# Scan products of an S5/short-convolution layer: high and low parts side by side, two parts of four groups

## Chip, cores and metric

One core of a Trainium2 chip. The metric is the device time of one execution in microseconds (us). The kernel before ran three times: median 1619.18 us, 1614.2 to 1620.25.

## What is computed

One layer over 576 tokens (a prompt of 512 and eight samples of eight), model width 2048. An input projection gives eight streams. One of them, u (1024 wide, 64 groups of 16 channels), drives a state space with 64 complex states per group; the other parts are a gated convolution and gates. Cut to what matters here:

```python
proj = jnp.einsum('bld,dn->bln', x, w_in)
u_a, z_a, b_c, c_c, h_c, z_c, g_a, g_c = jnp.split(proj, SPLIT_POINTS, axis=-1)
bu = einsum('blgc,gpc->blgp', u_groups, b_bar)          # input to the states
h = associative_scan(...)                               # h_t = lam * h_(t-1) + bu_t
y = einsum('blgp,gcp->blgc', h_re, c_re) - einsum('blgp,gcp->blgc', h_im, c_im) + d * u
y = gelu(y); y = y * sigmoid(y @ w_glu)
merged = sigmoid(g_a) * ((y * silu(z_a)) @ w_out_a) + sigmoid(g_c) * (conv_part @ w_out_c)
y_out = layernorm(alpha * x + merged @ w_o)
```

## The kernel before

**Main products.** Every float32 product is made of three in the one-pass type float32r: with high and low parts of both sides, hi*hi, hi*lo and lo*hi are added in PSUM. The weights come as 264 "halves" (128 output features by 1024 inputs; the last 32 pass a second time). Per half h, SyncE loads `w_raw`, ScalarE copies the high part (`split`, L736), VectorE subtracts to get the low part (`split`, L947), and TensorE issues 48 matmuls of 288 columns (`half`, L618: 8 blocks of 128 inputs, 3 products, 2 token halves). `lo_ready` lets TensorE into a half, `half_done` is incremented at its end, and ScalarE and VectorE run their own copies of the loop over h. In step h each of them first makes the parts of half h + 2, then reads the accumulator of the half that ends with this step (if its turn comes), and only then does the scan's steps: `scan_steps(h)` stands last in every iteration. An engine's queue is strictly in program order.

**The scan.** The 64 groups go in 8 blocks of 8 groups. Tokens are cut in chunks of T = 8, so a block's tokens are 72 columns per group. A block b begins every 16 halves, and `ssm_step(h, off)` says at which distance `off` from a block's begin a step falls. The blocks run beside halves 16 to 159: the first 64 of these are the convolution's (L1293, four blocks begin there), the next 16 the gate z_a's (L1328), the last 64 the merge gates' (L1341). Of a block:

- off 4, 5: high and low parts of the matrices and of u (`lcl` L1204, `lbl` L1210, `ul` L1213);
- off 7, before half 7: TensorE's `states_in` (L637 to L639), for each group lbh*uh, lbh*ul and lbl*uh of 72 columns into `v_ps`, 24 in all, then 16 narrow ones for the filter taps (L646); ScalarE copies `v_ps` to `v_st` (L774) in its step 7; VectorE goes on with it in step 8 (`chunk_sums`);
- off 9 to 17: rotation, scan, rotation back, high and low parts of the states (`hh`, `hl`);
- off 19, before half 19: TensorE's `outputs` (L658 to L663), six products of 72 columns per group into `y_ps`, 48 in all; ScalarE copies `y_ps` to `y_pre` (L757);
- off 20 to 24: GELU on VectorE and ScalarE (L1228, L1229, L792, L1233), and the store.

The accumulator readers that matter: in the convolution, at off 3 and 11 (mod 8: 3) VectorE waits for `half_done(h + 1)`, the end of the half that is running, and makes q (L1304 to L1308); at 5 (mod 8) it waits likewise and multiplies (L1318); at 7 (mod 8) ScalarE makes the sigmoid (L831) and VectorE two products (L1323, L1325), again after that half's end. In z_a's halves, every odd h has ScalarE's sigmoid (L841) and VectorE's product (L1335) after the half's end; in the merge gates' halves every odd h has ScalarE's sigmoid (L854) there, and VectorE has nothing of the kind.

Of the kernel before, what the change touches and what calls it, by code (L numbers as in the profile page):

```python
# [5 lines left out]
F32 = mybir.dt.float32  # L6
# [88 lines left out]
def build(nc, d):  # L95
# [52 lines left out]
    u_raw = r("u_raw", [P, NG, CH])  # L148
    uh = r("uh", [P, NG, CH], F32R)
    ul = r("ul", [P, NG, CH], F32R)  # L150
    lbh = r("lbh", [P, NG, 2 * STATE], F32R)
# [12 lines left out]
    y_pre = r("y_pre", [P, NG, CH])  # L164
    hh = r("hh", [P, NG, CH], F32R)
    hl = r("hl", [P, NG, CH], F32R)
    k_st = r("k_st", [P, 2, T * GC])
# [8 lines left out]
    out_st = [r(f"out_st{i}", [P, TOK]) for i in range(4)]  # L176
    st = u_raw

    r = Region(s0)
# [57 lines left out]
    def halves_of(ps):  # L237
        return ps[:, :, 0:TH]
# [17 lines left out]

    def by_bank(t):
        return t[:, :, :].rearrange("p (t g) n -> p t (g n)", t=2)

# [41 lines left out]
    k_done = sem("k_done")  # L301
    v_evac = sem("v_evac")
    k_evac = sem("k_evac")
    v_ready = sem("v_ready")
# [11 lines left out]
    y_done = sem("y_done")  # L316
    y_evac = sem("y_evac")
    y_arg = sem("y_arg")
    y_sig = sem("y_sig")
# [195 lines left out]
    def _(pool):  # L515
# [56 lines left out]
        def scan_moves(h):  # L572
            if (b := ssm_step(h, -1)) is not None:
                load_mats(b)
            if (b := ssm_step(h, 2)) is not None:
                load_u(b)
            if (b := ssm_step(h, 9)) is not None:
                pool.wait_ge(v_ready, b + 1)
                swap(v_sw, v_st, v_swapped)
            if (b := ssm_step(h, 12)) is not None:  # L580
                pool.wait_ge(s_ready, b + 1)
                swap(v_sw, v_st, s_swapped)
            if (b := ssm_step(h, 11)) is not None:
                store_k(b)
            if (b := ssm_step(h, 13)) is not None:
                load_lt(b)
            if (b := ssm_step(h, 24)) is not None:
                store_y(b)

        store_mq()  # L590
        for h in range(SSM0 - 1, SSM0 + SSM_PER * (BLK - 1) + 25):
            scan_moves(h)

    @blk.tensor
    def _(pe):
# [30 lines left out]
        def out_of(ps, g):  # L626
            t, at = divmod(g * CH, TH)
            return ps[:, t, at:at + CH]

        def states_in(b):  # L630

            pe.wait_ge(lbl_ready, b + 1)
            pe.wait_ge(ul_ready, b + 1)
            if b:
                pe.wait_ge(v_evac, b)
            for g in range(NG):
                ins = pe.matmul(out_of(v_ps, g), lbh[:, g, :], uh[:, g, :], start=True, stop=False)  # L637
                ins = pe.matmul(out_of(v_ps, g), lbh[:, g, :], ul[:, g, :], start=False, stop=False)  # L638
                ins = pe.matmul(out_of(v_ps, g), lbl[:, g, :], uh[:, g, :], start=False, stop=True)  # L639
            ins.then_inc(v_done, 1)  # L640
            pe.wait_ge(lc_ready, b + 1)
            if b:
                pe.wait_ge(y_evac, b)
# [6 lines left out]
        def outputs(b):  # L650
            pe.wait_ge(hl_ready, b + 1)
            pe.wait_ge(lcl_ready, b + 1)
            pe.wait_ge(lt_loaded, LT_LOAD * (b + 1))
            pe.wait_ge(k_evac, b + 1)
            for g in range(NG):
                o = out_of(y_ps, g)
                ch, cl = (t[:, g, :, :].rearrange("p t c -> p (t c)") for t in (lch, lcl))
                pe.matmul(o, lth[:, g, :], uh[:, g, :], start=True, stop=False)  # L658
                pe.matmul(o, lth[:, g, :], ul[:, g, :], start=False, stop=False)  # L659
                pe.matmul(o, ltl[:, g, :], uh[:, g, :], start=False, stop=False)  # L660
                pe.matmul(o, ch, hh[:, g, :], start=False, stop=False)  # L661
                pe.matmul(o, ch, hl[:, g, :], start=False, stop=False)  # L662
                ins = pe.matmul(o, cl, hh[:, g, :], start=False, stop=True)  # L663
            ins.then_inc(y_done, 1)
# [63 lines left out]
    def _(act):  # L728
# [23 lines left out]
        def scan_steps(h):  # L752
            if (b := ssm_step(h, 19)) is not None:
                act.wait_ge(y_done, b + 1)
                if b:
                    act.wait_ge(y_stored, U_LOAD * b)
                act.activation(by_bank(y_pre), halves_of(y_ps), ACT.Copy).then_inc(y_evac, 1)  # L757
            if (b := ssm_step(h, 3)) is not None:
                act.wait_ge(lc_ready, b + 1)
                if b:  # L760
                    act.wait_ge(y_done, b)
                act.activation(lch[:, :, :, :].rearrange("p g t c -> p g (t c)"),
                               lc[:, :, 1:, :].rearrange("p g t c -> p g (t c)"), ACT.Copy).then_inc(lch_ready, 1)
            if (b := ssm_step(h, 4)) is not None:
                act.wait_ge(lb_ready, b + 1)
                act.activation(lbh[:, :, :], mb[:, :, :, :].rearrange("p g c s -> p g (c s)"), ACT.Copy)\
                   .then_inc(lbh_ready, 1)
                act.wait_ge(u_loaded, U_LOAD * (b + 1))
                act.activation(flat(uh), flat(u_raw), ACT.Copy).then_inc(uh_ready, 1)
            if (b := ssm_step(h, 7)) is not None:  # L770
                act.wait_ge(v_done, b + 1)
                if b:
                    act.wait_ge(st_ready, b)
                act.activation(by_bank(v_st), halves_of(v_ps), ACT.Copy).then_inc(v_evac, 1)  # L774
# [5 lines left out]
            if (b := ssm_step(h, 9)) is not None:  # L780
                act.wait_ge(kd_ready, b + 1)
                if b:
                    act.wait_ge(k_stored, 32 * b)
                act.activation(k_hi[:, :, :], k_st[:, :, :], ACT.Copy).then_inc(kh_ready, 1)
            if (b := ssm_step(h, 15)) is not None:
# [3 lines left out]
                act.activation(hh[:, :, CP:], h0[:, 0, b * NG:(b + 1) * NG, :], ACT.Copy).then_inc(hh_ready, 1)  # L789
            if (b := ssm_step(h, 21)) is not None:  # L790
                act.wait_ge(y_arg, b + 1)
# [144 lines left out]
    def _(dve):  # L936
# [227 lines left out]
        def chunk_sums(b):  # L1164
            dve.wait_ge(v_evac, b + 1)
            dve.tensor_tensor(v_st[:, :, CP:], v_st[:, :, CP:], w0[:, b * NG:(b + 1) * NG, :], ALU.add)\
# [23 lines left out]
        def scan_steps(h):  # L1190
# [9 lines left out]
            if (b := ssm_step(h, 2)) is not None:  # L1200
                output_matrix(b)
            if (b := ssm_step(h, 4)) is not None:
                dve.wait_ge(lch_ready, b + 1)
# [3 lines left out]
                                  ALU.subtract).then_inc(lcl_ready, 1)  # L1207
            if (b := ssm_step(h, 5)) is not None:
                dve.wait_ge(lbh_ready, b + 1)
                dve.tensor_tensor(lbl[:, :, :], mb[:, :, :, :].rearrange("p g c s -> p g (c s)"),  # L1210
                                  lbh[:, :, :].bitcast(F32), ALU.subtract).then_inc(lbl_ready, 1)
                dve.wait_ge(uh_ready, b + 1)
                dve.tensor_tensor(flat(ul), flat(u_raw), flat(uh).bitcast(F32), ALU.subtract).then_inc(ul_ready, 1)  # L1213
            if (b := ssm_step(h, 8)) is not None:
                chunk_sums(b)
            if (b := ssm_step(h, 10)) is not None:
                dve.wait_ge(kh_ready, b + 1)
# [12 lines left out]
            if (b := ssm_step(h, 22)) is not None:  # L1230
                dve.wait_ge(y_sig, b + 1)
# [321 lines left out]
```

## Time and profile before

| | |
|---|---|
| median of three runs | 1619.18 us (1614.2 to 1620.25) |
| profiled execution | 1611.43 us, its span 1609.6 us |
| busy in the span | TensorE 98%, VectorE 51%, ScalarE 28%, GpSimd 12% |
| mean granted TensorE clock | 0.984 of full |
| DMA | 221 MB, mean 137 GB/s |

The span runs from the first to the last instruction. Busy time of TensorE counts overlapping matmuls once, and a matmul's row lasts longer than the distance to the next one, so costs of matmuls are read below from distances between starts. A granted clock of 1.00 is 2.4 GHz, 0.50 is 1.2 GHz.

### The profile page before, as it was taken

The numbers are of one execution on the slowest core, as the hardware profiler recorded it, in microseconds if no ns is written. First come the engines' busy times: TensorE is split into PE (matmuls) and PEld (weight loads), VectorE is DVE, ScalarE is ACT, GpSimd is POOL, SyncE is SP. The second block draws the span as 40 slices with busy tenths as digits, with TensorE's granted clock in tenths as the row PEclk, the third lists the DMA queues.
The fourth block names the chain that finished last, engine by engine and source line by source line (L and its number), as shares of the span: only waits on it lengthen the run. The fifth ranks groups of instructions, "written<-read, shape, count | busy, mean of one in ns | idle before, by whom it ended". The sixth has DMA issues, their size and how long they took to land.

```text
span 1609.6 us, 27311 instructions
## 1 busy us (share of the span) xinstructions
PE 1576.2 (98%) x11878; PEld 1571.0 (98%) x11878; DVE 820.9 (51%) x1148; ACT 443.2 (28%) x566; POOL 189.0 (12%) x348
## 2 busy tenths in 40 slices
PE   8999999999999999999999999999999999999994
PEld 8999999999999999999999999999999999999993
DVE  5976374464463563543533523123742355566887
ACT  4222222222222222222222222222421122333444
POOL 0110041131211311212212212010000000000000
PEclk9999999999999999999999999999999999999997
DMA  9352262352443543534634535244544433456572
GB/s 306 100 162 92 88 173 74 110 150 70 134 117 101 137 122 111 166 99 125 174 97 140 150 84 160 81 145 157 182 143 131 132 123 116 157 184 194 184 224 101
DMA packets 87448, 221.23 MB, mean 137 GB/s; under 512 B 19744, under 2 KB 28576, under 8 KB 87328
## 3 DMA queue, kind: packets, MB, share of 16 engines
q1 hardware_dynamic: 71456, 188.78, 37.1%
q0 software_dynamic: 15872, 30.70, 8.1%
q8 instruction: 93, 1.52, 0.4%
q14 instruction: 27, 0.22, 0.0%
HBM read 186.55 MB, written 28.16 MB: 133 GB/s over the span
## 4 chain that ended last, share of the span: by engine, by line
PE 93%; DVE 5%; SPq 1%; DMA 1%; issue 1%; ACT 0%; DVEq 0%
PE acc L618 88%; DVE w_lo L947 1%; SPq L404 1%; DMA w_raw<-in_w 1%; PE y_ps L662 0%; PE y_ps L663 0%; PE y_ps L661 0%; DVE r_all L1437 0%; PE y_ps L660 0%; PE y_ps L659 0%; PE v_ps L638 0%; PE v_ps L639 0%; PE v_ps L637 0%; PE y_ps L658 0%; DVE r_all L1436 0%
## 5 line engine op out<-in xcount | busy, mean ns | idle before, releaser
L618 PE MATMUL acc<-xh,w_hi 128*128 128x288 f32 x2560 | 556.0, 298 | 5.6 <-DVE xl L955 3.3
L618 PE MATMUL acc<-xl,w_hi 128*128 128x288 f32 x2560 | 553.4, 297 | 0.0
L618 PE MATMUL acc<-xh,w_lo 128*128 128x288 f32 x2560 | 552.5, 297 | 0.0
L947 DVE TENSOR_TENSOR w_lo<-w_raw,w_hi 128x1024 fp32r<-128x1024 f32 x263 | 321.6, 1224 | 408.1 <-ACT w_hi L736 406.5
L736 ACT ACTIVATE w_hi<-w_raw 128x1024 fp32r<-128x1024 f32 x263 | 277.8, 1058 | 607.3 <-PE acc L618 592.5
L618 PEld LDWEIGHTS acc<-xh,w_hi 128*128 128x128 f32 x2560 | 414.7, 190 | 8.1 <-issue 4.3
L618 PEld LDWEIGHTS acc<-xh,w_lo 128*128 128x128 f32 x2560 | 415.3, 190 | 0.0
L618 PEld LDWEIGHTS acc<-xl,w_hi 128*128 128x128 f32 x2560 | 415.2, 190 | 0.0
L618 PE MATMUL acc<-mh,w_hi 128*128 128x288 f32 x512 | 151.4, 296 | 0.0
L618 PE MATMUL acc<-mh,w_lo 128*128 128x288 f32 x512 | 150.7, 294 | 0.0
L618 PE MATMUL acc<-ml,w_hi 128*128 128x288 f32 x512 | 150.7, 294 | 0.0
L618 PEld LDWEIGHTS acc<-ml,w_hi 128*128 128x128 f32 x512 | 96.0, 188 | 0.2
L618 PEld LDWEIGHTS acc<-mh,w_hi 128*128 128x128 f32 x512 | 96.0, 188 | 0.2
L618 PEld LDWEIGHTS acc<-mh,w_lo 128*128 128x128 f32 x512 | 96.0, 188 | 0.0
L854 ACT ACTIVATE out_st<-acc 128x576 f32<-128x576 f32 x32 | 20.9, 654 | 205.5 <-PE acc L618 205.5
L570 POOL DMA_DIRECT2D y_dram<-y_pre x64 | 33.6, 532 | 294.6 <-DVE y_pre L1233 274.4
L618 PE MATMUL acc<-gcl,w_hi 128*128 128x288 f32 x256 | 55.0, 296 | 0.0
L618 PE MATMUL acc<-gch,w_lo 128*128 128x288 f32 x256 | 55.0, 296 | 0.0
L618 PE MATMUL acc<-gah,w_hi 128*128 128x288 f32 x256 | 55.0, 296 | 0.0
L618 PE MATMUL acc<-gal,w_hi 128*128 128x288 f32 x256 | 55.0, 296 | 0.0
L618 PE MATMUL acc<-gah,w_lo 128*128 128x288 f32 x256 | 55.0, 296 | 0.0
L618 PE MATMUL acc<-gch,w_hi 128*128 128x288 f32 x256 | 55.0, 296 | 0.0
(272 smaller groups left out, 1543.8 us busy)
## 6 DMA issues: line engine op xcount, KB each, us to landing
w_raw<-in_w SPq DMA_DIRECT2D x263, 512.0 KB, 3.8
sg_dram<-out_st SPq DMA_DIRECT2D x32, 288.0 KB, 4.5
v_sw<-v_st POOLq DMA_DIRECT2D x32, 144.0 KB, 4.9
gc_in<-sg_dram SPq DMA_DIRECT2D x16, 288.0 KB, 2.7
sz_in<-sg_dram SPq DMA_DIRECT2D x16, 288.0 KB, 2.8
x_in<-in_xT SPq DMA_DIRECT2D x32, 144.0 KB, 2.2
outT<-o_st SPq DMA_DIRECT2D x32, 144.0 KB, 1.8
mb<-mq_dram POOLq DMA_DIRECT2D x8, 512.0 KB, 6.9
```

The source lines that it names most:

```text
L404: sp.dma_start(k_dram[part, b, :, :, 0:KROW - T * GC].rearrange("x p n -> p x n"), zeros[:, :, :]).then_inc(zeros_stored, 16)
L570: pool.dma_start(dst[j], y_pre[GC * j:GC * j + GC, :, :]).then_inc(y_stored, 16)
L618: ins = pe.matmul(acc[:, par, t, 0:TH], w, m[:, k0 + k, t * TH:(t + 1) * TH], start=first and k == 0 and n == 0, stop=last and k == KH - 1 ...
L736: act.activation(w_hi[h % NW][:, :], w_raw[:, h % NW, :], ACT.Copy).then_inc(hi_ready, 1)
L854: act.activation(two(out_st[n % 4][:, :]), halves_of(acc[:, n % 2]), ACT.Sigmoid).then_inc(g_sig, 1)
L947: dve.tensor_tensor(w_lo[h % NW][:, :], w_raw[:, h % NW, :], w_hi[h % NW][:, :].bitcast(F32), ALU.subtract).then_inc(lo_ready, 1)
```

## The change

High and low parts of u lie side by side in one tile, `u2` [group, part, 72], and of the states in `h2`. One matmul streams both parts, 144 columns, against the high matrix and one against the low matrix (lo*lo is thus added too, which the kernel before left out). The result has two halves of 72 columns, the products with the high and the low part, which must be added: ScalarE copies one half out of PSUM, VectorE adds the other from PSUM (new semaphores `v_sum`, `y_sum`). A group now takes 144 columns of PSUM instead of 72, so eight do not fit into the two banks, and both TensorE steps are cut in two parts of four groups: the second part reuses the first's columns and comes one half later, after the first part's sum. The steps between are moved by one half.

```diff
+        def states_in(b, part):
+            if part == 0:
+                pe.wait_ge(lbl_ready, b + 1)
+                pe.wait_ge(ul_ready, b + 1)
+            if b or part:
+                pe.wait_ge(v_sum, 2 * b + part)
+            for g in range(4 * part, 4 * part + 4):
+                u = u2[:, g, :, :].rearrange("p x n -> p (x n)")
+                pe.matmul(out_of(v_ps, g), lbh[:, g, :], u, start=True, stop=False)
+                ins = pe.matmul(out_of(v_ps, g), lbl[:, g, :], u, start=False, stop=True)
             ins.then_inc(v_done, 1)
...
+        def outputs(b, part):
+            if part == 0:
+                pe.wait_ge(hl_ready, b + 1)
...
+            else:
+                pe.wait_ge(y_sum, 2 * b + 1)
+            for g in range(4 * part, 4 * part + 4):
...
+                pe.matmul(o, lth[:, g, :], u, start=True, stop=False)
+                pe.matmul(o, ltl[:, g, :], u, start=False, stop=False)
+                pe.matmul(o, ch, v, start=False, stop=False)
+                ins = pe.matmul(o, cl, v, start=False, stop=True)
             ins.then_inc(y_done, 1)
...
             if (b := ssm_step(h, 7)) is not None:
-                states_in(b)
+                states_in(b, 0)
+                taps(b)
+            if (b := ssm_step(h, 8)) is not None:
+                states_in(b, 1)
             if (b := ssm_step(h, 19)) is not None:
-                outputs(b)
+                outputs(b, 0)
+            if (b := ssm_step(h, 20)) is not None:
+                outputs(b, 1)
```

On ScalarE, in `scan_steps`, the copy of `v_ps` (off 7) and of `y_ps` (off 19) becomes two of half the size, off 7 and 8, 19 and 20. On VectorE:

```diff
+            for part, off in enumerate((7, 8)):
+                if (b := ssm_step(h, off)) is not None:
+                    dve.wait_ge(v_evac, 2 * b + part + 1)
+                    v = part_of(v_st, part)
+                    dve.tensor_tensor(v, v, of_part(v_ps, 1), ALU.add).then_inc(v_sum, 1)
+            for part, off in enumerate((19, 20)):
+                if (b := ssm_step(h, off)) is not None:
+                    dve.wait_ge(y_evac, 2 * b + part + 1)
+                    y = part_of(y_pre, part)
+                    dve.tensor_tensor(y, y, of_part(y_ps, 1), ALU.add).then_inc(y_sum, 1)
-            if (b := ssm_step(h, 4)) is not None:
+            if (b := ssm_step(h, 5)) is not None:
                 dve.wait_ge(lch_ready, b + 1)
...
-            if (b := ssm_step(h, 5)) is not None:
+            if (b := ssm_step(h, 6)) is not None:
                 dve.wait_ge(lbh_ready, b + 1)
...
-            if (b := ssm_step(h, 20)) is not None:
-                dve.wait_ge(y_evac, b + 1)
+            if (b := ssm_step(h, 21)) is not None:
+                dve.wait_ge(y_sum, 2 * b + 2)
```

The order of the instructions shows where these land. **VectorE around off 7 of the first block**, of the kernel before (L1323 and L1325 are the convolution's products after the end of half 7, `w_lo` is the split for the half two on):

```order
L1323 TENSOR_TENSOR gate_t<-gate_t,acc 128x576 [waits z_sig,half_done]
L1325 TENSOR_TENSOR conv_t_91<-conv_t_91,gate_t 128x576 [waits dve_step]
L947 TENSOR_TENSOR w_lo<-w_raw,w_hi 128x1024 [waits hi_ready]
L1166 TENSOR_TENSOR v_st<-v_st,w_52 128x8x8 [waits v_evac]
L1169 TENSOR_TENSOR k_st<-k_st,ddiag 128x2x16 [waits k_evac]
```

and of the changed one, where L1353 and L1355 are the same two products and L1226 is the new sum (once per part):

```order
L1353 TENSOR_TENSOR gate_t<-gate_t,acc 128x576 [waits z_sig,half_done]
L1355 TENSOR_TENSOR conv_t_89<-conv_t_89,gate_t 128x576 [waits dve_step]
L1226 TENSOR_TENSOR v_st<-v_st,v_ps 128x288 [waits v_evac]
L967 TENSOR_TENSOR w_lo<-w_raw,w_hi 128x1024 [waits hi_ready]
L1226 TENSOR_TENSOR v_st<-v_st,v_ps 128x288 [waits v_evac]
```

The first sum stands behind the two products that wait for `half_done`; TensorE's second part waits for it (`v_sum`).

**VectorE around off 19 of the first block**, changed kernel (L1334 to L1338 are the convolution's q after the end of half 19, L1231 the new sums; L1348 and what follows is off 21, which is off 5 of the next block):

```order
L1334 COPY q_pad<-conv_par 128x2x8 [waits half_done,cc_ready,conv_last]
L1335 TENSOR_TENSOR q_pad<-gate_t,acc 128x576
L1338 COPY q_pad<-q_pad 128x2x63 [waits dve_step]
L1231 TENSOR_TENSOR y_pre<-y_pre,y_ps 128x288 [waits y_evac,dve_step]
...
L1231 TENSOR_TENSOR y_pre<-y_pre,y_ps 128x288 [waits y_evac,dve_step]
L967 TENSOR_TENSOR w_lo<-w_raw,w_hi 128x1024 [waits hi_ready]
L1348 TENSOR_TENSOR conv_t_89<-conv_t_89,acc 128x576 [waits half_done]
L1234 TENSOR_TENSOR lcl<-lc,lch 128x1024 [waits dve_step,lch_ready]
L1258 SCALAR_TENSOR_TENSOR scr_77<-y_pre 128x576 [waits lc_ready,y_sum]
L1259 SCALAR_TENSOR_TENSOR scr_77<-scr_77,y_pre 128x576 [waits dve_step]
L967 TENSOR_TENSOR w_lo<-w_raw,w_hi 128x1024 [waits hi_ready]
L1240 TENSOR_TENSOR lbl<-mb,lbh 128x1024 [waits lbh_ready]
L1243 TENSOR_TENSOR u_69<-u_raw,u_69 128x8x72 [waits uh_ready]
```

and the kernel before from the same place of off 20 on:

```order
L1204 TENSOR_TENSOR lcl<-lc,lch 128x1024 [waits lch_ready,dve_step]
L1228 SCALAR_TENSOR_TENSOR scr_78<-y_pre 128x576 [waits lc_ready,y_evac]
L1229 SCALAR_TENSOR_TENSOR scr_78<-scr_78,y_pre 128x576 [waits dve_step]
L947 TENSOR_TENSOR w_lo<-w_raw,w_hi 128x1024 [waits hi_ready]
L1318 TENSOR_TENSOR conv_t_91<-conv_t_91,acc 128x576 [waits half_done]
L1210 TENSOR_TENSOR lbl<-mb,lbh 128x1024 [waits dve_step,lbh_ready]
L1213 TENSOR_TENSOR ul<-u_raw,uh 128x576 [waits uh_ready]
```

`lcl` and the two GELU operations moved behind the wait of L1318, and `lbl` and `ul` behind one more split; all of it now stands between the end of half 5 and the beginning of the states' products.

## Rows read from the trace of the kernel before

**Rows 1.** The page: busy time of each engine.
```profile
PE 1576.2 (98%) x11878; PEld 1571.0 (98%) x11878; DVE 820.9 (51%) x1148; ACT 443.2 (28%) x566; POOL 189.0 (12%) x348
```

**Rows 2.** TensorE's timeline at outputs, block 0: start us, us, instruction.
```profile
240.81 0.27 PE L659 MATMUL y_ps<-ul,lth 128*128 128x72 f32 x1
...
245.61 0.28 PE L660 MATMUL y_ps<-uh,ltl 128*128 128x72 f32 x1
...
246.09 0.41 PE L663 MATMUL y_ps<-hh,lcl 128*128 128x72 f32 x1
246.30 0.83 PE L618 MATMUL acc<-xh,w_hi 128*128 128x288 f32 x2
...
249.28 0.42 PE L618 MATMUL acc<-xh,w_hi 128*128 128x288 f32 x2
```

**Rows 3.** The warm-up matmuls of 224 columns, by line.
```profile
L669 PE MATMUL y_ps<-zeros 128*128 128x224 f32 x26 | 5.9, 419 | 1.2 <-DVE zeros L958 1.2
```

**Rows 4.** Windows: stretch, its us, busy us of each engine (x), PEclk, DMA share, GB/s.
```profile
90.20:92.50 2.30, 2.30 (x18) 2.30 (x19) 2.03 (x9) 0.00 (x0) 0.00 (x0) 1.00 0.87 171
...
240.80:245.70 4.90, 4.90 (x47) 4.90 (x46) 3.28 (x5) 1.06 (x1) 0.00 (x0) 1.00 0.20 41
245.70:249.20 3.50, 3.50 (x17) 3.50 (x17) 0.00 (x0) 1.60 (x2) 0.00 (x0) 0.51 0.31 119
...
1119.60:1123.00 3.40, 3.04 (x13) 3.07 (x14) 1.49 (x2) 0.42 (x1) 0.00 (x0) 0.50 0.51 156
```

**Rows 5.** Timeline of all engines at the end of half 7, block 0.
```profile
170.38 0.43 PE L618 MATMUL acc<-xh,w_hi 128*128 128x288 f32 x2
...
170.58 0.65 ACT L831 ACTIVATE gate_t<-acc 128x576 f32<-128x576 f32 x1 [8.63 <-PE acc L618]
...
173.03 1.23 DVE L947 TENSOR_TENSOR w_lo<-w_raw,w_hi 128x1024 fp32r<-128x1024 f32 x1
```

**Rows 6.** Lines of 288 columns that read PSUM: VectorE and ScalarE.
```profile
L1396 DVE SCALAR_TENSOR_TENSOR r_all<-x_in,acc 128x288 f32<-128x288 f32 x32 | 14.5, 452 | 14.3 <-PE acc L618 14.1
...
L898 ACT ACTIVATE mean<-v_ps 128x288 f32<-128x288 f32 x2 | 0.8, 402 | 0.9 <-PE v_ps L704 0.9
```

**Rows 7.** TensorE's longest idle times: timeline, idle time before in brackets.
```profile
90.16 0.50 PE L618 MATMUL acc<-xh,w_hi 128*128 128x288 f32 x2 [2.04 <-DVE w_lo L947]
...
1119.96 0.82 PE L618 MATMUL acc<-yh,w_hi 128*128 128x288 f32 x2 [2.38 <-issue]
```

**Rows 8.** VectorE's timeline, first operation after the chain at 1119.
```profile
1119.10 0.76 DVE L1347 TENSOR_TENSOR yl<-y_in,yh 128x576 fp32r<-128x576 f32 x1 [5.34 <-ACT yh L846]
```

**Rows 9.** VectorE's timeline after the end of half 19, block 0.
```profile
254.37 0.18 DVE L1304 COPY q_pad<-conv_par 128x16 f32<-128x16 f32 x1 [10.21 <-PE acc L618]
...
255.69 1.22 DVE L947 TENSOR_TENSOR w_lo<-w_raw,w_hi 128x1024 fp32r<-128x1024 f32 x1
```

**Rows 10.** Timelines of ScalarE and VectorE after an odd half of z_a's.
```profile
605.01 0.65 ACT L841 ACTIVATE out_st<-acc 128x576 f32<-128x576 f32 x1 [5.28 <-PE acc L618]
...
606.67 1.23 DVE L1210 TENSOR_TENSOR lbl<-mb,lbh 128x1024 fp32r<-128x1024 f32 x1
```

**Rows 11.** ScalarE's timeline after half 7 of block 5, in the merge gates' halves.
```profile
733.83 0.66 ACT L854 ACTIVATE out_st<-acc 128x576 f32<-128x576 f32 x1 [8.65 <-PE acc L618]
734.65 0.65 ACT L774 ACTIVATE v_st<-v_ps 128x576 f32<-128x576 f32 x1 [0.17 <-ACT out_st L854]
```

**Rows 12.** VectorE's timeline, off 20 to 22 of block 0, which is off 4 to 6 of block 1.
```profile
259.09 1.22 DVE L1204 TENSOR_TENSOR lcl<-lc,lch 128x1024 fp32r<-128x1024 f32 x1
...
261.82 1.23 DVE L947 TENSOR_TENSOR w_lo<-w_raw,w_hi 128x1024 fp32r<-128x1024 f32 x1
...
267.97 1.23 DVE L1210 TENSOR_TENSOR lbl<-mb,lbh 128x1024 fp32r<-128x1024 f32 x1
...
269.78 1.22 DVE L947 TENSOR_TENSOR w_lo<-w_raw,w_hi 128x1024 fp32r<-128x1024 f32 x1
```

**Rows 13.** TensorE's timeline, beginning of block 1's states.
```profile
273.27 0.20 PE L637 MATMUL v_ps<-uh,lbh 128*128 128x72 f32 x1
```

More of the change, by code:

```diff
@@ L177, in build @@
     st = u_raw
+    uh, ul = (u2[:, :, i, :] for i in range(2))
+    hh, hl = (h2[:, :, i, :] for i in range(2))
     r = Region(s0)
@@ L302, in build @@
     v_evac = sem("v_evac")
+    v_sum = sem("v_sum")
     k_evac = sem("k_evac")
@@ L317, in build @@
     y_evac = sem("y_evac")
+    y_sum = sem("y_sum")
     y_arg = sem("y_arg")
@@ L586, in scan_moves @@
                 load_lt(b)
-            if (b := ssm_step(h, 24)) is not None:
+            if (b := ssm_step(h, 25)) is not None:
                 store_y(b)
         store_mq()
-        for h in range(SSM0 - 1, SSM0 + SSM_PER * (BLK - 1) + 25):
+        for h in range(SSM0 - 1, SSM0 + SSM_PER * (BLK - 1) + 26):
             scan_moves(h)
@@ L626, in out_of, with taps @@
         def out_of(ps, g):
[L627 to L639, printed above, removed]
+            t, at = divmod(g % 4 * 2 * CH, 4 * CH)
+            return ps[:, t, at:at + 2 * CH]
+        def states_in(b, part):
[8 more added lines that the diff above has]
+                ins = pe.matmul(out_of(v_ps, g), lbl[:, g, :], u, start=False, stop=True)
             ins.then_inc(v_done, 1)
+        def taps(b):
             pe.wait_ge(lc_ready, b + 1)
             if b:
-                pe.wait_ge(y_evac, b)
+                pe.wait_ge(y_sum, 2 * b)
             for g in range(NG):
@@ L648, in states_in @@
             ins.then_inc(k_done, 1)
[L650 to L655, printed above, removed]
+        def outputs(b, part):
+            if part == 0:
+                pe.wait_ge(hl_ready, b + 1)
+                pe.wait_ge(lcl_ready, b + 1)
+                pe.wait_ge(lt_loaded, LT_LOAD * (b + 1))
+                pe.wait_ge(k_evac, b + 1)
+            else:
+                pe.wait_ge(y_sum, 2 * b + 1)
+            for g in range(4 * part, 4 * part + 4):
                 o = out_of(y_ps, g)
                 ch, cl = (t[:, g, :, :].rearrange("p t c -> p (t c)") for t in (lch, lcl))
[L658 to L663, printed above, removed]
+                u, v = (t[:, g, :, :].rearrange("p x n -> p (x n)") for t in (u2, h2))
+                pe.matmul(o, lth[:, g, :], u, start=True, stop=False)
+                pe.matmul(o, ltl[:, g, :], u, start=False, stop=False)
+                pe.matmul(o, ch, v, start=False, stop=False)
+                ins = pe.matmul(o, cl, v, start=False, stop=True)
             ins.then_inc(y_done, 1)
@@ L752, in scan_steps @@
         def scan_steps(h):
[L753 to L758, printed above, removed]
+            for part, off in enumerate((19, 20)):
+                if (b := ssm_step(h, off)) is not None:
+                    act.wait_ge(y_done, 2 * b + part + 1)
+                    if b:
+                        act.wait_ge(y_stored, U_LOAD * b)
+                    act.activation(part_of(y_pre, part), of_part(y_ps, 0), ACT.Copy).then_inc(y_evac, 1)
+            if (b := ssm_step(h, 4)) is not None:
                 act.wait_ge(lc_ready, b + 1)
                 if b:
-                    act.wait_ge(y_done, b)
+                    act.wait_ge(y_done, 2 * b)
                 act.activation(lch[:, :, :, :].rearrange("p g t c -> p g (t c)"),
                                lc[:, :, 1:, :].rearrange("p g t c -> p g (t c)"), ACT.Copy).then_inc(lch_ready, 1)
-            if (b := ssm_step(h, 4)) is not None:
+            if (b := ssm_step(h, 5)) is not None:
                 act.wait_ge(lb_ready, b + 1)
@@ L768, in scan_steps @@
                 act.wait_ge(u_loaded, U_LOAD * (b + 1))
-                act.activation(flat(uh), flat(u_raw), ACT.Copy).then_inc(uh_ready, 1)
+                act.activation(uh, u_raw[:, :, :], ACT.Copy).then_inc(uh_ready, 1)
+            for part, off in enumerate((7, 8)):
+                if (b := ssm_step(h, off)) is not None:
+                    act.wait_ge(v_done, 2 * b + part + 1)
+                    if b:
+                        act.wait_ge(st_ready, b)
+                    act.activation(part_of(v_st, part), of_part(v_ps, 0), ACT.Copy).then_inc(v_evac, 1)
             if (b := ssm_step(h, 7)) is not None:
[L771 to L774, printed above, removed]
                 act.wait_ge(k_done, b + 1)
@@ L779, in scan_steps @@
                    .then_inc(k_evac, 1)
-            if (b := ssm_step(h, 9)) is not None:
+            if (b := ssm_step(h, 10)) is not None:
                 act.wait_ge(kd_ready, b + 1)
@@ L1201, in scan_steps @@
                 output_matrix(b)
-            if (b := ssm_step(h, 4)) is not None:
+            for part, off in enumerate((7, 8)):
+                if (b := ssm_step(h, off)) is not None:
+                    dve.wait_ge(v_evac, 2 * b + part + 1)
+                    v = part_of(v_st, part)
+                    dve.tensor_tensor(v, v, of_part(v_ps, 1), ALU.add).then_inc(v_sum, 1)
+            for part, off in enumerate((19, 20)):
+                if (b := ssm_step(h, off)) is not None:
+                    dve.wait_ge(y_evac, 2 * b + part + 1)
+                    y = part_of(y_pre, part)
+                    dve.tensor_tensor(y, y, of_part(y_ps, 1), ALU.add).then_inc(y_sum, 1)
+            if (b := ssm_step(h, 5)) is not None:
                 dve.wait_ge(lch_ready, b + 1)
@@ L1229, in scan_steps @@
                 dve.scalar_tensor_tensor(s, s, 1.0, y, ALU.add, ALU.mult).then_inc(y_arg, 1)
-            if (b := ssm_step(h, 22)) is not None:
+            if (b := ssm_step(h, 23)) is not None:
                 dve.wait_ge(y_sig, b + 1)
```

22 lines of the change are left out of this document (11 added, 11 removed).

## The prediction

> **What bounds the kernel.** I read the page first: TensorE is busy for 1576.2 us of a span of 1609.6, in 11878 matmuls, 133 ns each, nearly all of them the main products of 288 columns; VectorE is at 51%, ScalarE at 28% [rows 1]. The reader is to see that a microsecond saved on TensorE is a microsecond of the kernel, and a microsecond that TensorE waits is one too: no other engine has to be relieved. Its idle time is small, and the two longest waits of the middle are 2.0 and 2.4 us [rows 7]. Then I read TensorE's timeline where the scan's products run, the granted clock of those stretches, and last what ScalarE and VectorE do just after the end of the half in which the change puts its new wait.
>
> **What the products cost.** In `outputs` the starts of the 72-column matmuls go from 240.81 to 245.61 us in 43 steps [rows 2]: 111 ns each. A main product of four times the columns costs 133 ns. So these matmuls don't pay for columns. The warm-up, ahead of all others, says the same: 26 matmuls of 224 columns, in 5.9 us less the last one's 0.4 us, come 0.22 us apart [rows 3], and the last 72-column one, at half clock, takes 0.21 us to the next start (246.09 to 246.30) [rows 2]. The fixed part, most likely the weights that each matmul loads, ends last up to at least 224 columns. I take 111 ns for 144 columns; the bounds are 111 and 133 ns. A block goes from 24 + 48 = 72 such matmuls to 16 + 32 = 48. 24 x 0.111 = 2.67 us, times 8 blocks: **-21.3 us**. At 133 ns it would be 72 x 0.111 - 48 x 0.133 = 1.6 us per block, -12.9 us.
>
> The Trainium skill speaks against this step (TensorE: Matmul & The Clock Gate, Back-to-back issue gap): the distance between matmuls is the columns divided by the clock plus 2.5 ns, 32.5 ns for 72 columns and 62.5 for 144, an estimate from the page. By that rule 48 wide ones would take 3.0 us where 72 narrow ones took 2.3, a loss of 5 us in all. Rows 2 and 3 say that its premise fails here: 111 ns, not 32.5.
>
> **The clock before.** The granted clock is 1.00 in the 4.9 us of `outputs` at 240.8 and 0.51 in the 3.5 us behind them [rows 4]; this happens after each of the eight `outputs`. The cost: from 246.30 to 249.28 us 12 main matmuls run in 2.98 us instead of 1.60, and four steps ahead of them took 0.69 instead of 0.44: 1.63 us, times 8 = 13.1 us. The change cuts `outputs` into two runs of 16 matmuls, 1.8 us each, with a half between, and each streams twice the columns. I take it that these falls go: **-13.1 us**, between 0 and -13.1.
>
> **The new wait.** The second part may not start before the first part's sum, one half earlier. That sounds like 6.4 us of slack, but the sum stands last in VectorE's step, behind operations that wait for the end of that very half. The half between the parts therefore hides nothing: TensorE idles from the half's end until the sum is done. All sixteen second parts follow a half with such a reader. What the sum itself costs: 128x288 from PSUM takes VectorE 0.45 us [rows 6], and 0.1 us later TensorE starts (`yl` ends at 1119.86, TensorE starts at 1119.96) [rows 7, 8]. TensorE is free 0.20 us before ScalarE's sigmoid starts [rows 5].
> - `states_in`, convolution (4 blocks): TensorE could go on at 170.38; sigmoid, two products, and VectorE is free at 173.03 [rows 5]. 173.03 + 0.45 + 0.1 = 173.6: 3.2 us, times 4 = 12.8.
> - `outputs`, convolution (3): the half ends for TensorE at about 254.15; copy, product, copy, VectorE free at 255.69 [rows 9]; 256.25, so 2.1 us, times 3 = 6.3.
> - z_a's halves (1 of each kind): sigmoid at 605.01, so TensorE free at 604.8; VectorE free at 606.67 [rows 10]; 607.2: 2.4 us, times 2 = 4.8.
> - merge gates' halves (3 `states_in`, 4 `outputs`): sigmoid at 733.83, the scan's copy at 734.65 [rows 11], 0.40 us for half its size [rows 6], sum, 0.1: 735.6 to 735.7 against 733.63: 2.05 us, times 7 = 14.4.
>
> Together **+38.3 us**. VectorE's 32 more operations of 0.45 us and ScalarE's 16 more beside these are covered by their idle time.
>
> **The crowded step.** Between the end of half 5 and the states' products VectorE now has `lcl` and two GELU operations (259.09 to 261.82: 2.73 us), a split (1.14) and `lbl` with `ul` (267.97 to 269.78: 1.81) [rows 12]. From 267.97 on, where it is free after the convolution's product, that ends at about 273.75, plus 0.1; TensorE wants it at 273.27 [rows 13]. 0.6 us for blocks 1 to 3, and 1.3 us for block 4, whose queue is free only at 606.67 (606.67 + 2.73 + 1.14 + 1.89 + 0.1 = 612.5 against 604.8 + 48 x 0.133 = 611.2). Block 0 has no GELU ahead and later blocks no wait of VectorE on the half's end. **+3.1 us.** The other steps moved by one half (`chunk_sums`, `k_hi`, the store) have a half or more to spare, and GpSimd's queue keeps its order but for the store, which now goes behind the next block's swap.
>
> **The clock after.** TensorE idled 2.38 us before 1119.96 (2.67 between starts), and the clock fell to 0.50 from 1119.6 on; after 2.04 us of idling before 90.16 it stayed at 1.00 behind them [rows 4, 7]. The new waits lie at these and beyond, and a sparse run of narrow matmuls follows each. I take all four waits of 3.2 us and half of the twelve of 2.05 to 2.4: 10 falls of 1.63 us, **+16.3 us**; bounds 0 and 16 falls (26.1 us).
>
> **The sum.** -21.3 - 13.1 + 38.3 + 3.1 + 16.3 = +23.3 us. The profiled execution took 1611.43 us (span 1609.6, 1.8 around it), so 1634.7 on its scale. The median of the runs is 7.8 us above that execution, and I set the prediction on the median's scale: 1619.2 + 23.3 = 1642.5, say 1642.
>
> **The rivals.**
> 1. *The sums are in time* (0.06, faster). The wait decides only if VectorE and ScalarE reach the first sum before half 7 or 19 ends; the point is whether the reader's wait stands ahead of it in the queue. If the sum came inside the half, nothing of 38.3 nor of the falls after it remains: -21.3 - 13.1 + 3.1 = -31.3, 1588 us. For it: VectorE is idle 8 to 10 us ahead of these readers [rows 9]. Against it: the order of the queue, which shows the sum behind L1353, L1355 and L1338, and the copy of `v_ps` in the kernel before, which already ran behind the sigmoid [rows 11].
> 2. *Waits, but no fall of the clock* (0.10). Stretches of 2 us idling left it up once. Then +7.0 us, 1626; with waits a tenth shorter, +3, within half a per cent.
> 3. *The clock falls after every wait* (0.12): 16 falls, +33.1, 1652.
> 4. *The change saves little* (0.04): 144 columns cost 133 ns instead of 111: +8.4 on the forecast, 1651. The Trainium skill's rule above points this way.
>
> **The numbers.** The forecast, with 3 to 15 falls, has 0.68. The range must take in rivals 2 to 4 with the spread of the runs (5 us below the median, 1 above): 1619.2 + 7.0 - 4 = 1622, and 1652 + 8.4 = 1660. A change of 0.5%, 8 us, is about what a measurement can tell from none. Faster 0.06 is rival 1; the same 0.08 is most of rival 2; slower is the rest, 0.86.
>
> **What would show it.** The waits of TensorE name `v_st` and `y_pre` sums of VectorE, 16 of them, of 3.2, 2.1, 2.4 and 2.05 us, about 38 us; the 144-column matmuls start 111 ns apart; granted clock 1.00 behind the first parts and 0.50 for a stretch behind several second parts, a mean near 0.98 as before; small waits for `ul` in blocks 1 to 4. I am wrong if the waits are far below 2 us, if the starts are 133 ns apart, or if the clock hardly falls.

## The result, and the profile after

| | before | changed |
|---|---|---|
| median | 1614.2 us (1612.35 to 1620.25, 5 runs) | 1641.88 us (1635.02 to 1656.98, 5 runs) |
| ratio of the runs | | 1.0175, 95% interval 1.0146 to 1.0204 |
| profiled execution, its span | 1611.43, 1609.6 us | 1656.98, 1655.2 us |
| mean granted clock there | 0.984 | 0.970 |

The change makes the kernel slower, by 27.7 us between the medians. The profiled execution is the slowest of the five; the others had a mean clock of 0.979 to 0.983 and took 1635 to 1644 us.

The page's line on busy time, to be read beside [rows 1], shows 192 matmuls less and a smaller share for TensorE:

```profile
PE 1582.6 (96%) x11686; PEld 1571.9 (95%) x11686; DVE 833.4 (50%) x1180; ACT 445.6 (27%) x582; POOL 188.9 (11%) x348
```

TensorE's waits in the changed kernel (waited for: us in total, times, longest):

```profile
PE v_ps L646 <- DVE v_st L1226: 19.1, 8, 2.9
PE y_ps L672 <- DVE y_pre L1231: 15.7, 8, 2.3
...
PE v_ps L646 <- DVE lbl L1240: 1.0, 1, 1.0
```

Sixteen new waits for the two sums. The timelines at the first (block 0, off 8) show the chain; TensorE:

```profile
170.95 0.43 PE L625 MATMUL acc<-xh,w_lo 128*128 128x288 f32 x2
174.25 0.49 PE L646 MATMUL v_ps<-u,lbh 128*128 128x144 f32 x1 [2.87 <-DVE v_st L1226]
...
174.96 0.41 PE L647 MATMUL v_ps<-u,lbl 128*128 128x144 f32 x1
...
175.81 0.41 PE L647 MATMUL v_ps<-u,lbl 128*128 128x144 f32 x1
176.03 0.78 PE L625 MATMUL acc<-xh,w_hi 128*128 128x288 f32 x2
```

ScalarE:

```profile
171.42 0.65 ACT L851 ACTIVATE gate_t<-acc 128x576 f32<-128x576 f32 x1 [6.89 <-PE acc L625]
171.97 0.41 ACT L793 ACTIVATE v_st<-v_ps 128x288 f32<-128x288 f32 x1
```

VectorE:

```profile
172.17 0.76 DVE L1353 TENSOR_TENSOR gate_t<-gate_t,acc 128x576 f32<-128x576 f32 x1 [6.38 <-ACT gate_t L851]
173.07 0.76 DVE L1355 TENSOR_TENSOR conv_t<-conv_t,gate_t 128x576 f32<-128x576 f32 x1
173.75 0.45 DVE L1226 TENSOR_TENSOR v_st<-v_st,v_ps 128x288 f32<-128x288 f32 x1
```

Sigmoid, product, product, sum, and only then TensorE, exactly the row of operations that [rows 5] suggested. VectorE had been idle for 6.4 us before it, with its sum's input long in PSUM. ScalarE's copy, which the sum waits for, stood behind its own reader (the sigmoid, L851) in the same way. Counted from the end of the half to the next matmul (the distance between the two starts, less the usual 0.13), the waits cost 3.0 (states, convolution), 2.1 to 2.4 (outputs, convolution), 2.4 (z_a) and 2.0 us (merge gates), 37.2 us together.

The matmuls of 144 columns at full clock, here in the fastest variant below, where none waits:

```profile
161.10 0.28 PE L647 MATMUL v_ps<-u,lbl 128*128 128x144 f32 x1
...
161.77 0.27 PE L647 MATMUL v_ps<-u,lbl 128*128 128x144 f32 x1
```

Six steps in 0.67 us: 112 ns each, as the 72-column ones of [rows 2] (43 steps in 4.80 us). At half clock the wide ones take 0.21 us: in the timeline above, from 174.96 to 175.81 in four steps.

The clock, by stretches (us; busy of each engine; PEclk; DMA share; GB/s), at five of the sixteen waits' ends in the changed kernel:

```profile
173.60:180.40 6.80, 6.15 (x26) 6.15 (x27) 2.19 (x4) 0.41 (x1) 0.00 (x0) 0.50 0.47 123
258.90:265.70 6.80, 6.80 (x31) 6.80 (x32) 3.42 (x5) 1.35 (x2) 0.00 (x0) 0.50 0.23 77
294.50:298.00 3.50, 3.50 (x28) 3.50 (x29) 2.10 (x3) 0.41 (x1) 0.00 (x0) 1.00 0.27 35
378.40:381.80 3.40, 3.40 (x16) 3.40 (x16) 1.72 (x3) 1.35 (x2) 0.00 (x0) 0.50 0.43 154
...
849.40:856.20 6.80, 6.80 (x32) 6.80 (x32) 1.68 (x2) 1.36 (x3) 0.00 (x0) 0.50 0.41 120
```

Some waits are followed by 3.4 us at half clock, some by 6.8, and some by none: at 294.5 the clock stays up behind a wait of 3.0 us. In all, (1 - 0.970) x 2 x 1655.2 = 99 us of this execution ran at half clock. 20.7 of them lie in the end, where TensorE is done, and 3.4 each at 91.6 and 1166.8, outside the scan; some 72 us are left, in twelve falls (nine of 6.8 us, three of 3.4). The kernel before had 27 us (eight stretches of 3.4).

How the stretch of the scan is made up, TensorE's busy time first, of before and of the changed kernel:

```profile
100.00:1117.00 1017.00, 1017.00 (x7733) 1015.05 (x7733) 453.88 (x549) 240.09 (x306) 178.38 (x325) 0.99 0.42 122
```

```profile
100.00:1162.00 1062.00, 1024.96 (x7557) 1017.58 (x7556) 467.36 (x585) 243.34 (x323) 178.30 (x325) 0.97 0.42 117
```

TensorE had no idle time in the scan, and now has 37.0 us (34.8 of it is the view's figure for the sixteen waits; by the distances between starts, as above, they cost 37.2). Of the 45.6 us between the two spans, the sum in the prediction's terms is: products -21.3, sixteen waits +37.2, smaller waits for the low part of u +3.4, clock +21.3 (44 us more at half clock, each of which costs 0.48 us by [rows 2]). That is 40.6. Of the other 5.0 us, 2.7 come ahead of the scan: TensorE was 1.1 us later when its wait for a weight's low part ended at 91 us (90.16 before, 91.23 now), and the clock fell behind that wait (1.6). The remaining 2.3 us lie within the scan, and their cause is open. They are there in the fastest form below too: from the end of that wait to the first GLU half it takes 995.4 us where the kernel before takes 1027.1, 31.7 less and not the 34.4 of the two savings.

### The profile page after: what moved, and what is told of

Same layout as the page of the kernel before. It is cut to its first block, busy times and chain, and to the rows that moved or that the text cites. A ratio compares the mean times of both kernels' runs of the same rounds, so it can differ in the third digit from the quotient of the medians.

```text
span 1655.2 us, 26989 instructions
## 1 busy us (share of the span) xinstructions
PE 1582.6 (96%) x11686; PEld 1571.9 (95%) x11686; DVE 833.4 (50%) x1180; ACT 445.6 (27%) x582; POOL 188.9 (11%) x348
## 4 chain that ended last, share of the span: by engine, by line
PE 89%; DVE 6%; SPq 1%; issue 1%; ACT 1%; DMA 1%; DVEq 0%; ACTq 0%
PE acc L625 85%; DMA w_raw<-in_w 1%; DVE w_lo L967 1%; PE v_ps L646 1%; PE y_ps L672 1%; SPq L411 1%; PE y_ps L675 1%; PE y_ps L674 1%; PE y_ps L673 1%; DVE r_all L1467 0%; PE v_ps L647 0%; DVE r_all L1466 0%; ACT out_st L874 0%; PE y_ps L656 0%; DVE y_pre L1231 0%
## 5 line engine op out<-in xcount | busy, mean ns | idle before, releaser
L625 PE MATMUL acc<-xh,w_hi 128*128 128x288 f32 x2560 | 561.7, 301 | 7.7 <-DVE w_lo L967 4.4
L625 PEld LDWEIGHTS acc<-xh,w_hi 128*128 128x128 f32 x2560 | 419.9, 193 | 10.3 <-issue 6.5
L625 PEld LDWEIGHTS acc<-xl,w_hi 128*128 128x128 f32 x2560 | 420.3, 193 | 0.0
L555 POOL DMA_DIRECT2D v_sw<-v_st x32 | 18.3, 576 | 510.8 <-DVE v_st L1186 482.1
```

The costliest lines, as they stand in the source:

```text
L555: pool.dma_start(to[64 * x:64 * x + 64, :, :], of[64 - 64 * x:128 - 64 * x, :, :]).then_inc(done, 16)
L625: ins = pe.matmul(acc[:, par, t, 0:TH], w, m[:, k0 + k, t * TH:(t + 1) * TH], start=first and k == 0 and n == 0, stop=last and k == KH - 1 ...
```

## Experiments

The theory: the cost is in the order of two queues. The sum that TensorE needs after one half stands, on VectorE and ScalarE, behind work that waits for the end of that half; and idling there brings the clock down. Rivals: the wide products cost more than taken, or the falls of the clock come from the products and not from the waits. Each variant was timed beside the kernel before, whose median was 1613 to 1614 us in every set, so that the medians can be set side by side.

### The changed kernel again

> The changed kernel again, beside the others on one chip. 27 us slower than the kernel before in both theories; 16 waits for the sums, 37 us together, in any profile. Theory (idle time of TensorE brings the clock down): the stretches at half clock differ from run to run, since how a wait lies to them differs, so its time scatters more (5 to 20 us) than that of the kernel before. Rival (the falls come from the products themselves): the same falls at the same places in each profile.

1639.72 us (1630.21 to 1646.79), ratio 1.0155 (1.0103 to 1.0206). The waits are the same to a tenth (19.1 and 15.7 us), the clock is not:

```profile
174.20:177.60 3.40, 3.40 (x16) 3.40 (x16) 1.08 (x2) 0.41 (x1) 0.00 (x0) 0.50 0.52 102
258.00:262.00 4.00, 4.00 (x34) 4.00 (x33) 2.62 (x5) 1.36 (x2) 0.00 (x0) 1.00 0.39 131
372.20:379.00 6.80, 6.80 (x31) 6.80 (x31) 2.90 (x5) 1.35 (x2) 0.00 (x0) 0.50 0.23 77
```

Half as long at 174, not at all at 258, where the first execution had 6.8 us. Its clock of 0.981 over 1628.4 us is 34 us at half clock in the scan (eight falls, two of them of 6.8 us) against 72. In the merge gates' halves the first execution had a fall behind each of the four waits of `outputs` and none behind the three of `states_in`; this one had falls behind two of those three and one of the four, with the same waits of 2.0 us. So the waits are this kernel's fixed part, and the clock is most of its scatter.

It is not all of it. The spans of the two profiled executions differ by 26.8 us, of which the clock explains 18 (38 us at half clock, 0.48 each). Another 6.6 lie behind the scan, from the first GLU half to the end: 489.6 against 483.0 us, with the same wait of 2.4 us, one fall of 3.4 us and a mean clock of 0.98 in both. The execution of 1630.21 us is the fastest of this kernel's four, and its matmuls there start 131.0 ns apart where every other profiled execution of this document has 132.9, at the same granted clock. Why is open. Of three later forms, too, one run lies 5 to 7 us below the rest while its mean clock does not differ, so a difference of that size between two single runs shows nothing.

### Sums ahead of the readers

The edit on VectorE; ScalarE's copies of the first parts move in the same way, and `early` is called in all three loops of the scan's stretch.

```diff
+        def early(h):
+            for part, off in ((0, 19),):
...
+                    dve.tensor_tensor(y, y, of_part(y_ps, 1), ALU.add).then_inc(y_sum, 1)
+            for part, off in ((0, 7),):
...
+                    dve.tensor_tensor(v, v, of_part(v_ps, 1), ALU.add).then_inc(v_sum, 1)
...
         for h in range(H_CONV, H_ZA):
             split(h + 2)
+            early(h)
```

> ScalarE's copy and VectorE's sum of the first parts (off 7 and off 19) stand ahead of the operations that wait for the end of the half; nothing else is changed. Theory (the queue's order makes the waits, and the waits make most of the falls of the clock): the 16 waits of 37 us vanish, 3 us of small waits for the low part of u stay, the clock falls hardly ever in the scan; -21.3 - 13.1 + 3 against the kernel before: 1583 us, about 59 below the changed one. Rival (runs of 144-column products bring the clock down without any wait): 16 falls of 1.6 us stay, about 1609 us. Second rival (the changed kernel's loss lies in the products, 133 ns or more each): 1592 us or more, with starts 133 ns apart.

1585.0 us (1578.51 to 1586.29), ratio 0.9811 (0.9774 to 0.9849): 55 us below the changed kernel, with the same instructions in another order. The scan's stretch:

```profile
100.00:1090.00 990.00, 987.74 (x7548) 984.10 (x7547) 466.16 (x585) 243.49 (x323) 177.52 (x325) 1.00 0.44 125
```

2.3 us idle instead of 37, and clock 1.00 throughout: 32 runs of wide products (sixteen of 8, sixteen of 16) without one fall. This strikes out both rivals. Both queues were changed together; how much each of the two, ScalarE's and VectorE's, would leave of the waits alone was not tried.

**One kind at a time.** The same edit for the states only, and for the outputs only.

> As the one with the sums first, but only for the states' products (off 7); the outputs' sum stays behind the readers. Theory (each wait and its fall of the clock is a thing of its own): the eight states' waits of 20.3 us and their falls (8 to 15 us) vanish, the outputs' eight waits of 17 us and their falls stay: about 1610 us. Rival (the waits hang together, and the one removed appears elsewhere, since VectorE is late anyway): 1635 us or more.

> The changed kernel with the sum ahead of the readers for the outputs only (off 19); the states' sum stays behind them. Theory (each wait and its fall is a thing of its own): the outputs' 16.9 us of waits go, and some of the falls; with the states-only one (-25 us) and both (-55 us) the difference should be near -30: 1610 us. Rival (the two hang together): 1625 us or more.

1615.01 us (1613.15 to 1616.1), ratio 1.0006 (0.9987 to 1.0025), and 1616.25 us (1609.37 to 1620.82), ratio 1.0014 (0.9996 to 1.0031). Against 1639.7 that is -24.7 and -23.5, 48 together, where both at once gave 54.7. In either profile only the removed waits are gone (the other line stands at 15.7 or 19.1 us as before), so the waits are separate things. The clock is not a sum of separate things: with eight waits there were still 34 and 31 us at half clock in the two profiles (seven falls each), as with sixteen in the second profile above (34). They recur at the same place of several blocks, 112.64 us apart (at 479.4, 592.1 and 704.7 with the states' sums first), which is what the eight falls of the kernel before did too.

### The waits filled with matmuls

```diff
+        def fill(par, n):
+            for _ in range(n):
+                pe.matmul(acc[:, par, 0, 0:TH], xh[:, 0, 0:P], xh[:, 1, 0:TH], start=True, stop=True)
...
             if (b := ssm_step(h, 8)) is not None:
+                fill(par, 21 if h < H_ZA else 16 if h < H_G else 14)
                 states_in(b, 1)
```

> The changed kernel with matmuls of 288 columns, whose results nobody reads, put into each of the 16 waits (21, 15, 16 or 14 of them, 133 ns each, a little less than the wait lasts). The waits stay as long as they are, but TensorE does not idle. Theory (idle time brings the clock down): the stretches at half clock in the scan vanish almost wholly, and the time is 1614 - 21 - 13 + 41 = 1621 us, some 20 below the changed kernel. Rival (the clock falls because of the products of 144 columns): the falls stay, 1640 us as the changed kernel.

1621.88 us (1620.55 to 1623.22, 10 runs), ratio 1.0048 (1.0033 to 1.0063); 17.8 us below the changed kernel. TensorE and the scan's stretch:

```profile
170.54 2.93 PE L680 MATMUL acc<-xh 128*128 128x288 f32 x21
173.57 0.34 PE L646 MATMUL v_ps<-u,lbh 128*128 128x144 f32 x1
```

```profile
100.00:1130.00 1030.00, 1026.81 (x7814) 1019.68 (x7813) 466.74 (x582) 242.89 (x322) 178.29 (x325) 1.00 0.41 120
```

The second part still begins 3.0 us after the half's end, but TensorE worked meanwhile, and the clock stays at 1.00 over the whole scan; all ten runs have a mean clock of 0.992 to 0.994. The scatter falls to 3 us. So what brought the clock down was the idling, and it was worth 18 us in a middling run; the 37 us of the waits themselves remain, and are all that remains: 1621.9 is 36.9 above the form with the sums first.

### The products by themselves

The changed kernel with its sums and waits, but 72-column products:

```diff
-                pe.matmul(out_of(v_ps, g), lbh[:, g, :], u, start=True, stop=False)
-                ins = pe.matmul(out_of(v_ps, g), lbl[:, g, :], u, start=False, stop=True)
+                o0, o1 = (out_of(v_ps, g)[:, i * CH:(i + 1) * CH] for i in range(2))
+                pe.matmul(o1, lbh[:, g, :], ul[:, g, :], start=True, stop=True)
+                pe.matmul(o0, lbh[:, g, :], uh[:, g, :], start=True, stop=False)
+                ins = pe.matmul(o0, lbl[:, g, :], uh[:, g, :], start=False, stop=True)
```

> The changed kernel with its parts, sums and waits, but with products of 72 columns as before, 24 and 48 a block, the low part's going to the other half of the columns. Theory (each product costs 111 ns whatever its columns): 192 more products of 111 ns, +21 us against the changed kernel, 1663 us. Rival (cost follows columns, the narrow ones are cheaper per product): within 10 us of it.

1673.85 us (1671.97 to 1676.46), ratio 1.038 (1.0338 to 1.0422): +34 where 21 was expected. The waits are the same 19.1 and 15.7 us; its mean clock in the scan is 0.96 against 0.98 of the second profile. The 21 us are the products, the rest fits the clock: the mean clock of its four runs is 0.970 to 0.975, that of the nine of the changed kernel 0.970 to 0.983 with a median of 0.979. The medians (0.9705 and 0.979) are 28 us at half clock apart, 13 us by the 0.48 above, and 21 + 13 is the 34 measured. So behind the same waits narrow products are followed by more time at half clock. The same products without any waits were then compared with the fastest form, which is described under "The fastest form".

> The fastest form so far (sums first, VectorE's steps spread) with products of 72 columns instead of 144: 24 and 48 a block instead of 16 and 32, all else equal, and no waits in either. Theory (a product of either width costs 111 ns): +21.3 us, 1600 us, plus 0 to 8 falls of the clock of 1.6 us since the runs are narrow again, up to 1613. Rival (much of the 34 us of that form comes from elsewhere, not from the count of the products): within 10 us of it, 1590 or less.

1603.1 us (1595.56 to 1603.78), ratio 0.9919 (0.9894 to 0.9943), against 1578.94 for the wide ones in the same set: 24 us for 192 matmuls. The clock in the scan is 1.00 for both; the narrow ones':

```profile
100.00:1105.00 1005.00, 1005.00 (x7724) 1003.06 (x7723) 466.45 (x587) 244.03 (x323) 177.90 (x325) 1.00 0.44 123
```

The two profiled executions can be compared more closely, since both have the same two falls of the clock outside the scan: their spans are 1601.9 and 1580.0, 21.9 us apart, and the stretch from 91 us to the first GLU half differs by 21.1. The first term was 21.3. The other 2 to 3 us are scatter of the runs.

### The falls of the kernel before

Outputs cut in two parts in the kernel before, without a wait between them:

```diff
-        def outputs(b):
+        def outputs(b, part):
...
-            for g in range(NG):
+            for g in range(4 * part, 4 * part + 4):
```

> The kernel before, only its outputs cut into two parts of four groups, the second one half later, with no wait between them (each group keeps its own columns); ScalarE's copy and the next block's lch come one step later. Same 72-column products, same count. Theory (a long run of narrow products brings the clock down, one of 24 does not): the eight falls after outputs vanish, -13 us: 1601 us. Rival (any run of narrow products does it, or the falls have to do with something else in that step): 1614 us.

1603.94 us (1599.91 to 1610.02, 10 runs), ratio 0.9942 (0.9922 to 0.9962): -10.0. Stretches of it:

```profile
163.40:166.80 3.40, 3.40 (x43) 3.16 (x42) 1.22 (x1) 1.06 (x1) 0.00 (x0) 1.00 0.09 36
166.80:170.20 3.40, 3.40 (x16) 3.40 (x16) 0.00 (x0) 0.00 (x0) 0.00 (x0) 0.50 0.48 154
240.00:250.00 10.00, 10.00 (x81) 10.00 (x80) 8.25 (x10) 1.72 (x2) 2.66 (x6) 1.00 0.35 94
```

The eight falls behind outputs are gone, but three new ones follow a run of 24 narrow products and taps in `states_in` (at 166.8, 279.5 and 392.1). So the theory held for outputs, and its second half, that a run of 24 does no harm, was wrong: the same run that left the clock up in the kernel before brought it down here in three blocks of eight. -13.1 + 3 x 1.63 = -8.2 fits the -10.0.

A run of wide products did it nowhere in the forms without waits. But neither did the narrow ones of the form with 72 columns and no waits above, whose states are cut in two parts as well, so that 12 products precede the taps instead of 24. So it is not the width that keeps the clock up in the scan; cutting both kinds of run in two was enough there, where all four runs have a mean clock of 0.991. No run here shows why a run of 24 with taps brings the clock down in one kernel and not in the other; that stays open.

### The fastest form

Sums ahead of the readers, and VectorE's steps spread again:

```diff
-            if (b := ssm_step(h, 5)) is not None:
+            if (b := ssm_step(h, 4)) is not None:
                 dve.wait_ge(lch_ready, b + 1)
...
-            if (b := ssm_step(h, 6)) is not None:
+            if (b := ssm_step(h, 5)) is not None:
                 dve.wait_ge(lbh_ready, b + 1)
...
-            if (b := ssm_step(h, 21)) is not None:
+            if (b := ssm_step(h, 20)) is not None:
                 dve.wait_ge(y_sum, 2 * b + 2)
```

> As the one with the sums first, and VectorE's steps that crowded between the end of half 5 and the states' products are spread again: lcl at off 4, the two GELU operations at off 20, lbl and ul at off 5. Theory: the small waits for the low part of u (3 us) vanish too: 1580 us, 3 below the other. Rival (VectorE has no room at off 4 and 20 either): no difference, 1583 us.

1579.08 us (1578.5 to 1580.21), ratio 0.9784 (0.9752 to 0.9816). VectorE and the scan's stretch:

```profile
162.38 1.23 DVE L984 TENSOR_TENSOR w_lo<-w_raw,w_hi 128x1024 fp32r<-128x1024 f32 x1 [3.62 <-ACT w_hi L753]
163.52 0.45 DVE L1237 TENSOR_TENSOR v_st<-v_st,v_ps 128x288 f32<-128x288 f32 x1
```

```profile
100.00:1085.00 985.00, 985.00 (x7539) 982.80 (x7539) 465.64 (x582) 241.63 (x322) 178.30 (x325) 1.00 0.44 126
```

The sum is done at 163.97, five microseconds before the half ends; TensorE does not idle once in 985 us. The median is 5.9 us below that of the form that only moved the sums; the runs overlap (1578.51 there is its lowest), and so do the intervals of the two ratios. The profiles say what the edit is worth: the small waits of 3.4 us are gone. The spans differ by more, 1584.4 against 1576.7, since the first has two falls of the clock outside the scan (3.3 us) and a longer wait at 91 us, which have nothing to do with the edit; the fastest form again, in a later set, has the same two falls and a span of 1580.0.

**The same fault elsewhere.** TensorE's wait of 2.4 us at the first GLU half [rows 7, 8] has the same form: ScalarE's `yh` behind a sigmoid that waits for the half's end.

```diff
         for h in range(H_G, H_GLU):
             split(h + 2)
             early(h)
+            if Y_LOAD < h <= Y_LOAD + NB:
+                y_high(h - Y_LOAD - 1)
             if h % 2:
...
             scan_steps(h)
-            if Y_LOAD < h <= Y_LOAD + NB:
-                y_high(h - Y_LOAD - 1)
```

> The fastest form with one more operation moved on ScalarE: in the merge gates' halves the high part of y (yh) stands ahead of the sigmoid that waits for the end of the half, so that the last one no longer keeps TensorE waiting at the first GLU half (2.4 us in every kernel so far). Theory (same fault, same cure): that wait of 2.4 us vanishes, -2.5 us against the fastest form. Rival (the wait hangs on another semaphore that ends just then, the weights' or the load of y): no difference.

> The fastest form again, on the same chip as the one with yh moved: 1579 us; 2.5 us above that one in the theory, equal in the rival.

1577.04 us (1575.93 to 1578.22), ratio 0.9768 (0.9751 to 0.9785), and 1578.94 us (1573.71 to 1581.84), ratio 0.9772 (0.9752 to 0.9793). By time they can't be told apart. By the profile the wait is gone; the longest of TensorE's waits, with the line of 2.4 us no longer among them:

```profile
PE acc L625 <- DVE xl L992: 3.9, 2, 2.1
PE acc L625 <- DVE w_lo L984: 3.8, 2, 3.1
PE v_ps L721 <- DVEq L1472: 1.8, 1, 1.8
```

With or without this last step it is the best version: 2.2 to 2.3% below the kernel before, 4% below the change as it was made.

## Why the prediction was right

1642 us was forecast, 1641.88 measured, within 1622 to 1660. Part of that closeness is luck: the forecast stood on the median of three runs, 1619.2, while more runs put the kernel before at 1614, so the difference was 27.7 where the sum had 23.3. The base was 5 us too high and the sum 4.4 too low. Of these 4.4, 2.3 are the time in the scan that no term names, 1.5 the clock after the waits and 0.3 the small waits; the sixteen waits were 1.1 less than forecast. The rest, 1.4, is within the scatter of the runs. By its steps:

- **Products, -21.3.** Right: 111 ns at 144 columns, and 192 fewer of them are worth 21 to 24 us with nothing else changed. The formula that the prediction took from the Trainium skill (TensorE: Matmul & The Clock Gate, Back-to-back issue gap) would have made this term a loss of 5, and the runs stand with the rows. The prediction also read that section too narrowly: it gives the formula for the gap of an isolated matmul, and for a stream of weight loads and matmuls about 81 ns at 128 columns. Neither is the 111 ns measured here. One support of the step is weaker than it was put: that the warm-up matmuls of 224 columns show the same fixed part supposes that they ran at half clock, and the granted clock has no record before 6.9 us of that execution. It can be worked out, since 0.22 us is more than the 133 ns of the wider 288 columns at full clock.
- **The falls after outputs, -13.1.** Right in effect: without waits the scan's clock is 1.00. Of its two reasons, two short runs and twice the columns, the second was not needed (72 columns, both kinds of run cut in two: 1.00), and the first is half the truth, since splitting the outputs alone let three falls move to the states.
- **The new wait, +38.3.** Right in mechanism and size: 37.2, every wait within 0.4 us of its own chain (3.0, 2.1 to 2.4, 2.4, 2.0), and moving the sums takes them away.
- **The crowded step, +3.1.** Right, 3.4: 0.4 for blocks 1 to 3 and 1.2 for block 4, where 0.6 and 1.3 were given. For blocks 5 to 7, which the working gave nothing, 0.3 each, of which the trace names only "issue"; that stays open.
- **The clock after, +16.3.** Near in size and partly by luck: the filled waits price it at 18 us in a middling run. The reasoning by length was too simple. "All four waits of 3.2 us and half of the twelve": in the profiled execution twelve of sixteen were followed by a fall, but one of the 3.0 us was not, and nine of the falls lasted 6.8 us instead of 3.4, some 72 us at half clock where ten times 3.4 was taken. In the second profile it was 34 us, with eight falls. How long a wait lasts does not say whether a fall follows.
- **The rivals.** The first, sums in time, is what the reordered form is: 1588 was given for it, 1585 measured. It failed as a forecast only by the queue's order, as argued. "A fall after every wait" (1652) is near what the slowest run, 1657, shows. 133 ns for a wide product is struck out.

## What to carry to other kernels

When a buffer is reused after one more step of a pipeline, ask what stands ahead of the releasing instruction in its engine's queue, not how long that instruction takes: a 0.45 us sum with 6.4 us of room cost 2 to 3 us sixteen times because readers of the running half's result stood before it. A wait on the bounding engine has a second price in the clock; it can be measured by filling the wait with idle work. And where many small matmuls all take the time of their fixed part, fewer and wider ones are a clear gain, if their result can leave PSUM in time.

## Not expected of the hardware

- 128x128 weights with 72 or 144 columns: 111 to 112 ns from start to start at 2.4 GHz, 0.21 us at 1.2 GHz; 288 columns take 133 ns and 0.24 us. At half clock the narrow ones nearly double too.
- A fall of the clock after a wait often lasts twice 3.4 us, most often when sixteen 144-column products follow the wait; they run at 0.21 us each and the clock stays down behind them (258.90 to 265.70 above). In the four profiles with waits and wide products, 12 of 17 falls behind a wait of `outputs` (sixteen products) lasted 6.8 us, and 4 of 17 behind one of `states_in` (eight).
- The same code has falls at other waits in each execution, with waits equal to a tenth of a microsecond: 1635 to 1657 us for one kernel. Where TensorE never idles (985 us of the fastest form), runs scatter by 2 us in one set of runs and by 8 in another, and the mean clock (0.990 to 0.993) does not say which run is the fast one.
